# First block's attention: row maxima, scaled negatives and reciprocals taken for two heads at once on VectorE

## The reference, cut to what matters

```
def block_attention(q, k, v):                       # per block of 128 query rows
    s = jnp.einsum('bqhgd,bkhd->bhgqk', qi, k, preferred_element_type=F32) * scale
    p = jax.nn.softmax(s, -1).astype(v.dtype)
    return jnp.einsum('bhgqk,bkhd->bqhgd', p, v)

q_l = apply_rope(rms_norm(aq_l...), cos, sin)       # latents: keys of latents and context, 512
att_l = block_attention(q_l, [k_l; k_c], [v_l; v_c])
if with_ctx_out:                                    # first layer only
    att_c = block_attention(q_c, k_c, v_c)          # context: keys of the context, 256
```

## Time and profile before

| | us |
|---|---|
| median of 3 runs | 1966.95 |
| lowest and highest | 1965.23, 1968.44 |
| profiled execution, its time | 1967.34 |
| its span in the trace | 1965.5 |

### The profile page before, as it was taken

One profiled execution on the slowest core, in us unless ns is written; L12 is line 12 of the kernel. 1 busy time (PEld: TensorE's weight loads), 2 busy tenths in 40 slices (PEclk: granted clock), 3 DMA queues, 4 the chain that ended last, 5 costly groups with the idle time before them and its releaser, 6 DMA issues.

```text
span 1965.5 us, 34448 instructions
## 1 busy us (share of the span) xinstructions
PE 1848.6 (94%) x15010; PEld 1629.9 (83%) x15010; DVE 1156.8 (59%) x1715; ACT 770.1 (39%) x1073; POOL 300.6 (15%) x264
## 2 busy tenths in 40 slices
PE   7999888999999978987999999999998999999998
PEld 5777556878888868856999999989988778899997
DVE  4643575554353337666655486555767778576654
ACT  4432563221122224455443443343455444344332
POOL 0011001899180010100000100002001111000000
PEclk9998998999999988999999999999999999999999
DMA  8344212565353222203555655544431111245551
GB/s 347 107 156 177 75 44 86 175 212 189 135 182 125 87 76 70 81 22 108 174 191 174 214 182 179 186 150 158 153 119 45 45 45 67 88 172 177 188 187 71
DMA packets 40759, 266.24 MB, mean 135 GB/s; under 512 B 4512, under 2 KB 4640, under 8 KB 13344
## 3 DMA queue, kind: packets, MB, share of 16 engines
q1 hardware_dynamic: 35712, 244.10, 35.5%
q0 software_dynamic: 4608, 16.78, 2.7%
q10 hardware_dynamic: 288, 3.15, 0.4%
HBM read 262.96 MB, written 1.05 MB: 134 GB/s over the span
## 4 chain that ended last, share of the span: by engine, by line
PE 75%; DVE 12%; POOL 5%; ACT 5%; issue 2%; DMA 2%; DVEq 0%; ACTq 0%; POOLq 0%
PE ps L641 18%; PE ps L643 18%; PE ps L642 18%; DVE W L621 2%; POOL work L1101 2%; PE ps L1641 2%; POOL work L1102 1%; PE ps L1003 1%; PE ps L647 1%; PE ps L1428 1%; PE ps L648 1%; PE ps L649 1%; PE ps L2372 1%; ACT W L612 1%; PE ps L2390 1%
## 5 line engine op out<-in xcount | busy, mean ns | idle before, releaser
L621 DVE TENSOR_TENSOR W<-ring,W 128x2048 fp32r<-128x2048 f32 (+2 forms) x194 | 439.5, 2267 | 247.2 <-ACT W L612 246.8
L612 ACT ACTIVATE W<-ring 128x2048 fp32r<-128x2048 f32 (+2 forms) x194 | 359.2, 1854 | 123.9 <-PE ps L643 114.0
L641 PE MATMUL ps<-h_lat,W 128*128 128x256 f32 x1056 | 301.4, 285 | 6.1 <-DVE h_lat L807 4.2
L643 PE MATMUL ps<-h_lat,W 128*128 128x256 f32 x1056 | 299.4, 283 | 0.0
L642 PE MATMUL ps<-h_lat,W 128*128 128x256 f32 x1056 | 299.4, 283 | 0.0
L641 PEld LDWEIGHTS ps<-h_lat,W 128*128 128x128 f32 x1056 | 203.2, 192 | 8.2 <-issue 4.6
L642 PEld LDWEIGHTS ps<-h_lat,W 128*128 128x128 f32 x1056 | 203.3, 193 | 0.3 <-issue 0.2
L643 PEld LDWEIGHTS ps<-h_lat,W 128*128 128x128 f32 x1056 | 203.3, 192 | 0.0
L748 POOL TENSOR_TENSOR work<-work 128x256 f32<-128x256 f32 (+1 forms) x42 | 41.1, 977 | 955.7 <-ACT work L730 768.5
L984 DVE TENSOR_TENSOR work<-work,ps 128x256 f32<-128x256 f32 (+1 forms) x88 | 43.0, 488 | 189.2 <-ACT work L959 189.1
L641 PE MATMUL ps<-hidden_lat,W 128*128 128x256 f32 x528 | 149.4, 283 | 0.0
(11 more groups left out here) (405 smaller groups left out, 4308.6 us busy)
## 6 DMA issues: line engine op xcount, KB each, us to landing
ring<-w_up_dram SPq DMA_DIRECT2D x88, 1024.0 KB, 4.9
ring<-w_down_dram SPq DMA_DIRECT2D x43, 1024.0 KB, 4.9
ring<-w_ada_dram SPq DMA_DIRECT2D x32, 1024.0 KB, 6.5
work<-w_ada_dram POOLq DMA_DIRECT2D x32, 512.0 KB, 4.1
ring<-w_rkv_dram SPq DMA_DIRECT2D x13, 1024.0 KB, 4.9
ring<-w_fm_dram SPq DMA_DIRECT2D x10, 1024.0 KB, 5.0
ring<-w_out_dram SPq DMA_DIRECT2D x8, 1024.0 KB, 4.9
ring<-w_gates_dram SPq DMA_DIRECT2D x16, 512.0 KB, 3.6
```

The source lines that it names most:

```text
L612: act.activation(slots[SLOT[s]][:, 0, 0:cols], ring[:, u % RING, 0:cols], ACT.Copy).then_inc(w_high, 1)
L621: dve.tensor_tensor(slots[SLOT[s]][:, 1, 0:cols], ring[:, u % RING, 0:cols], slots[SLOT[s]][:, 0, 0:cols], ALU.subtract).then_inc(w_low, 1)
L641: pe.matmul(o, slots[SLOT[s]][:, 0, at:at + cols], high, start=first, stop=False)
L643: return pe.matmul(o, slots[SLOT[s]][:, 1, at:at + cols], high, start=False, stop=final)
```

## The change

For each pair DVE waits for the scores of both units, takes both row maxima in one reduction over the two banks, and makes both scaled negatives in one SCALAR_TENSOR_TENSOR, which raises `at_max` by two. Then it waits for both exponentials of the pair before, takes both reciprocals in one instruction, and scales the two units' probabilities one after the other, as before in one instruction each.

```diff
-                if i < n:
-                    qt, j, b, nk = units[i]
-                    dve.wait_ge(at_s, base + i + 1)
-                    link(dve.tensor_reduce(at_small[:, 0, i:i + 1], ps[:, score_bank(i), 0:nk], AX, ALU.max))
-                    dve.tensor_scalar(at_small[:, 1, i:i + 1], at_small[:, 0, i:i + 1], qk_scale[:, j, qt, b:b + 1], -1.0,
-                                      ALU.mult, ALU.mult).then_inc(at_max, 1)
-                if 1 <= i <= n:
-                    x = i - 1
-                    dve.wait_ge(at_exp, base + x + 1)
-                    link(dve.reciprocal(at_small[:, 3, x:x + 1], at_small[:, 2, x:x + 1]))
-                    pr = probs[x % 4][:, 0:units[x][3]]
-                    dve.tensor_scalar(pr, pr, at_small[:, 3, x:x + 1], None, ALU.mult).then_inc(at_p, 1)
+                if i < n and i % 2 == 0:
+                    qt, j, _, nk = units[i]
+                    dve.wait_ge(at_s, base + i + 2)
+                    both = slice(i, i + 2)
+                    link(dve.tensor_reduce(at_small[:, 0, both], ps[:, score_bank(i):score_bank(i) + 2, 0:nk], AX, ALU.max))
+                    dve.scalar_tensor_tensor(out=at_small[:, 1, both], in0=at_small[:, 0, both], scalar=-1.0, in1=qk_scale[:, j, qt, :],
+                                             op0=ALU.mult, op1=ALU.mult).then_inc(at_max, 2)
+                if 2 <= i <= n and i % 2 == 0:
+                    dve.wait_ge(at_exp, base + i)
+                    link(dve.reciprocal(at_small[:, 3, i - 2:i], at_small[:, 2, i - 2:i]))
+                    for x in (i - 2, i - 1):
+                        pr = probs[x % 4][:, 0:units[x][3]]
+                        dve.tensor_scalar(pr, pr, at_small[:, 3, x:x + 1], None, ALU.mult).then_inc(at_p, 1)
```

## The result

| | before | changed kernel |
|---|---|---|
| median, us | 1965.14 | 1974.06 |
| lowest and highest | 1961.09 to 1971.94 | 1969.68 to 1983.25 |
| runs | 15 | 15 |
| span of the profiled execution | 1965.5 | 1972.1 |

The ratio is 1.0048 with a 95% interval of 1.0032 to 1.0063: the change costs some 9 us, between 6 and 12. The forecast was 0.47% slower.

What follows compares the result with a forecast made beforehand. An ACT and PE loop of 3.79 us was taken to pace 512-key rounds; late scalings would close a longer one through DVE. 5.1 us (first layer) plus 4.1 (second) gave 9.2, so 1976.1 us, 0.47% slower; 8-in-10 range 1971.5 to 1984.

Steps and rivals of the forecast that it cites:

- That the stage is on the path, and no transfer behind it takes up the delay: Both attention stages: a microsecond there is a microsecond of the whole; PE behind the first is busy 10.00 of 10.00 us.
- VectorE is not in the old loop: 512-key round before the change: the 3.79 us loop runs through ACT and PE; DVE sits idle 0.40 us.
- The new loop, 4.33 us for 512 keys: Ordinary 512-key rounds: scores, paired maxima, product, reciprocals, even scaling and transposes close a loop through DVE, 0.54 us longer.
- The new loop, 2.76 us for 256 keys: 256-key rounds: the same loop through DVE takes 2.76 us in place of 2.48, 0.28 more.
- The two rounds in which the kinds mix keep their old loop: First layer, two rounds mixing 512 and 256 keys: a short reduction meets long copies, so no growth.
- The split's round, 1.08 each: Round with the weight split, once per layer: both transposes wait for DVE, 3.17 in place of 2.09 us.
- The rival of the longer half clock: Behind each split: PE's low clock lasts one more round, about 2 us per layer, or more; 1980 to 1988, chance 0.14.
- The sum, 9.2 us: Both attention stages together: 5.1 us more in the first layer and 4.1 in the second.
- the four ordinary rounds: Second layer's attention: four 512-key rounds, counted with the way out as 5 x 0.54 = 2.7 us more.
- VectorE as the old bound: Rival: DVE's order held the old rounds, so 0.51 us returns in each of 24 pairs; 1955 to 1962, chance 0.05.
- The hidden delay: Rival: paired maxima cost no more than one (0.69), so the loop stays 3.79; 1967 to 1971, chance 0.09.
- The dearer reduction of two banks: Rival: paired reduction takes 1.38 us, 0.16 more per 512-key round, 2 us in all, 1978; inside the forecast's 0.72.

Runs made afterwards that it cites:

- the second trace: The changed kernel itself profiled and timed again, against the kernel before on the same chip: 1.0046 (1.0029 to 1.0064).
- the extra reduction: One more VectorE reduction of a constant per pair, behind the even unit's scaled negative: 1.0006 in the kernel before; 1.0072 with the change, against the kernel before.
- the low part late: Kernel before with VectorE's half of the weight split moved from its ninth step to behind the last unit's maximum: 0.9942, median 1953.94 us; same move with the change: 1.0000.
- paired reciprocals and the late low part: Kernel before with reciprocals paired between single maxima and VectorE's half of the weight split moved to the end: 0.9945 (0.9927 to 0.9964).

## Why the prediction was right

*That the stage is on the path, and no transfer behind it takes up the delay*: held. The stages are on the chain that ended last, as its pieces in order of time show. The shares of the earlier trace rows, with which the prediction argued, are shares of the whole span and do not place any work. Behind the stages the two traces of the change have from 2.9 us less to 2.1 more in each stretch than the one before, and in the second trace no stretch is longer.

*VectorE is not in the old loop*: held for the ordinary rounds, and tested by the extra reduction, which left them at 3.79 and 2.49 us. The rounds before and at the split did grow with it.

*The new loop, 4.33 us for 512 keys*: 4.37 measured. The reduction of 1024 columns took 1.22 us as taken from the one row out of SBUF, but 1.33 passed from its start to the next one's where 1.27 was put in, scores to reduction were 1.20 and not 1.16, and the reciprocals followed after 0.08 and not 0.13.

*The new loop, 2.76 us for 256 keys*: 2.88 measured, the worst of the two. From the reduction's start to the next were 0.80 us (265.42 to 266.22), not 0.73; and the row of the four transposes is 0.70 long where it was 0.66, and from their start to the scores passed 0.63, not 0.58. The odd unit's scaling, which was taken as hidden, probably shows through there.

*The two rounds in which the kinds mix keep their old loop*: held, 3.78 and 3.14 us where they were 3.78 and 3.13.

*The split's round, 1.08 each*: 1.5 and 1.4 measured (9.76 us from scores to scores in both layers, where they were 8.26 and 8.35). This term was priced with transposes at full clock. The prediction took 0.51 for the odd unit's, though its own rows have 1.04 from their start to the scores (242.00 to 243.04), and 1.03 for both units', which now took 1.89 (238.73 to 240.62): both stand at half clock where only the odd unit's did. The rival of the longer half clock came true in the first layer for part of one round: the value products behind the scores took 1.97 us too, where they had taken 1.10, and the next round was 5.32 us instead of 4.28. In the second layer that round was 5.32 both before and after. Against this rival the prediction had said that the clock came back within one round in the first layer; in the second it had not, in the kernel before already: PE ran at 0.50 from 877.60 to 882.57, 4.97 us. No later round ran at half clock, and the rival's 2 us more for each layer did not come.

*The sum, 9.2 us, against the runs*: 9 (6 to 12). Against the two traces of the change the stages grew by 12.4 and 12.1, some 3 us more than the sum, nearly all in the first layer (7.8 for 5.1). The terms that were too small there: the split's round by 0.4, the two rounds behind it by 0.8, the five rounds of 256 keys by 0.5, the start by 0.3 and the end by 0.5. At the start the second scores took 1.80 us in place of 1.13, at half clock, and at the end the last value products (1.12 for 0.66) and the first matmul of the output projection (0.79 for 0.51). Of the eight executions that came to the stage early, seven had the second scores for the most part at half clock (1.80 to 2.05 us); of the four that came late, none. The kernel before was profiled in a late one and the change twice in an early one. That can account for the start, some 0.3 us, and not for the rest of the 3. In the second layer terms that were too small and one that was too large partly cancelled: the four ordinary rounds, at 0.54 each, grew by 0.9, 0.8, 0.0 and 0.6. So the mechanism and the two round lengths were right, while it is in part luck that 9.2 came out so near to the runs' 9: the same sum done with the rounds as the traces have them gives 12, which is just inside the interval. Why traces and runs differ by 3 us stays open.

*The rivals.* VectorE as the old bound falls with the extra reduction. The hidden delay falls with the rounds. The dearer reduction of two banks falls: 1.22 us on average.

*The two halves of the Trainium skill's advice named ahead* (page "Perfetto Trace Analysis", section "Optimizing Scalar/DVE Operations"). Its first half says that grouping into larger operations can improve throughput if the engine is saturated. VectorE was not, being idle for 0.44 us in every round of the change, and still the order kept and the grouping taken away cost 12 us more. So what made grouping help was that VectorE stood in the loop. Its second half, that breaking up may complete the work sooner where the engine is not saturated and holds up others, came out in direction: the single instructions of the kernel before are 9 us faster. But breaking up alone made the change slower. It is the order that single instructions allow, and not their being single, that is worth the time here.

## What to carry to other kernels

Grouping instructions of two work items saves their fixed parts, but it also moves the first item's result behind the second item's work: before grouping, write down the closed loop of the round and see which engine waits for which half. Group what no one waits for between its halves (here the reciprocals, placed between the single maxima, cost next to nothing once the split was away) and keep single what another engine takes in turns. A long side job in such a stage is better put where its engine is idle anyway: moving 2.2 us of VectorE work in each layer to the stage's end brought 11 us, while no form of the grouping was faster than the kernel before.

## What the runs showed of the hardware

The length of a row is not its cost in a chain. A reduction of 256 columns out of SBUF with nothing waiting for it took 0.41 us and held up the next instruction for 0.33; the paired one out of PSUM, with `link` behind it, took 1.23 and held it up for 1.33. Over two banks of 256 columns the reduction was as long as over 512 columns of one bank (0.69 us), but from its start to the next passed 0.80 us in place of 0.73.

The granted clock of TensorE stayed at its upper level (2.4 GHz) through rounds of the change with 3.24 busy of 4.37 us. It fell to the lower (1.2 GHz) behind both splits of the kernel before and of the change, with 3.9 and 5.0 us of idleness, and did not fall in the first layer with the low part late, behind 1.28 us. One idleness alone does not tell it: at the start of the first stage, in the changed kernel, PE was busy for 1.31 of the 3.00 us from 214 to 217 at a clock of 1.00, the wait that ended there was 1.75 us, and the four us behind ran at 0.57. In the kernel with paired reciprocals and the late low part the same stretch (214.25 to 217.25, since that execution came 0.25 us later to it) also had 1.31 busy, and in the kernel before (219 to 222) it was 1.32; in both of these the four us behind ran at 1.00. So the same work ahead was followed by either level, and these traces do not show what decides it.
